# Gate and up chunks of the feed-forward in pairs, by seven block products in place of eight

## The reference

```python
def swiglu(h, w_gu, w_down):                 # h 256 x 1024, w_gu 1024 x 5632, w_down 2816 x 1024
    gate, up = jnp.split(h @ w_gu, 2, axis=-1)
    return (jax.nn.silu(gate) * up) @ w_down
x = x + 0.5 * swiglu(rmsnorm(x, ffn1_norm[i]), ffn1_w_gu[i], ffn1_w_down[i])
```

## Time and profile before

| | us |
|---|---|
| median of 3 runs | 2894.26 (2892.33 to 2895.02) |
| span of the profiled execution | 2891.6 |
| PE busy | 2851.9 |
| DVE busy | 1795.2 |
| ACT busy | 1578.0 |
| GpSimd busy | 452.6 |

### The profile page before, as it was taken

The page is one execution under the profiler, slowest core; times in us unless marked ns, Lnnn a source line. Parts: engine busy times, 40 slices in busy tenths (PEclk is TensorE's granted clock), DMA queues, the critical chain, the costliest instruction groups (busy, mean ns, idle before and its releaser), DMA issues.

```text
span 2891.6 us, 35970 instructions
## 1 busy us (share of the span) xinstructions
PE 2851.9 (99%) x14255; PEld 2419.0 (84%) x14255; DVE 1795.2 (62%) x2190; ACT 1578.0 (55%) x1982; POOL 452.6 (16%) x700
## 2 busy tenths in 40 slices
PE   9999999999999999999999999999999999999998
PEld 7888888888988888878888898888888888888887
DVE  5558666565666556466556487566675665775664
ACT  5448854544554454565444388643566463566462
POOL 1203512021002112041202107121000020000020
PEclk9999999999999999999999999999999999999999
DMA  8764267576548677537767653476645686645684
GB/s 277 234 191 129 88 218 239 195 247 214 173 155 245 214 227 238 181 117 225 227 207 241 200 159 117 133 247 212 200 147 174 214 278 220 194 146 176 217 278 158
DMA packets 397047, 574.90 MB, mean 199 GB/s; under 512 B 20016, under 2 KB 248624, under 8 KB 396880
## 3 DMA queue, kind: packets, MB, share of 16 engines
q1 hardware_dynamic: 372624, 508.62, 54.7%
q0 software_dynamic: 23680, 62.95, 7.0%
q10 hardware_dynamic: 576, 1.05, 0.1%
HBM read 540.03 MB, written 32.51 MB: 198 GB/s over the span
## 4 chain that ended last, share of the span: by engine, by line
PE 87%; DVE 6%; ACT 4%; issue 1%; DMA 1%; SPq 0%; POOL 0%; DVEq 0%; ACTq 0%
PE ps L430 26%; PE ps L432 26%; PE ps L431 26%; PE ps L616 2%; DVE lo L656 2%; DVE qkv L1609 2%; PE ps L503 1%; PE ps L505 1%; PE ps L504 1%; ACT goz L1400 1%; PE ps L587 1%; ACT hi L638 1%; PE ps L603 1%; ACT sl L1400 1%; ACT qkv L1400 0%
## 5 line engine op out<-in xcount | busy, mean ns | idle before, releaser
L656 DVE TENSOR_TENSOR lo<-raw,hi 128x2048 fp32r<-128x2048 f32 (+3 forms) x473 | 1052.6, 2238 | 451.0 <-ACT hi L638 451.0
L638 ACT ACTIVATE hi<-raw 128x2048 fp32r<-128x2048 f32 (+2 forms) x487 | 907.4, 1871 | 766.6 <-DMA raw<-in_ffn_w_gu 283.7
L430 PE MATMUL ps<-hi,xh 128*128 128x512 f32 (+1 forms) x2208 | 865.8, 392 | 3.3 <-DVE xl L812 2.4
L432 PE MATMUL ps<-hi,xl 128*128 128x512 f32 (+1 forms) x2208 | 858.4, 389 | 0.0
L431 PE MATMUL ps<-lo,xh 128*128 128x512 f32 (+1 forms) x2208 | 857.8, 388 | 0.0
L430 PEld LDWEIGHTS ps<-hi,xh 128*128 128x128 f32 x2208 | 415.0, 188 | 88.2 <-DVE lo L656 4.1
L432 PEld LDWEIGHTS ps<-hi,xl 128*128 128x128 f32 x2208 | 414.7, 188 | 85.8
L431 PEld LDWEIGHTS ps<-lo,xh 128*128 128x128 f32 x2208 | 415.1, 188 | 84.0 <-issue 1.0
L430 PE MATMUL ps<-hi,hhh 128*128 128x512 f32 x704 | 274.6, 390 | 0.0
L432 PE MATMUL ps<-hi,hhl 128*128 128x512 f32 x704 | 274.0, 389 | 0.0
L431 PE MATMUL ps<-lo,hhh 128*128 128x512 f32 x704 | 273.9, 389 | 0.0
(11 more groups left out here) (440 smaller groups left out, 3403.3 us busy)
## 6 DMA issues: line engine op xcount, KB each, us to landing
raw<-in_ffn_w_gu SPq DMA_DIRECT2D x348, 512.0 KB, 4.8
raw<-in_ffn_w_down SPq DMA_DIRECT2D x80, 1024.0 KB, 5.0
raw<-in_w_ff SPq DMA_DIRECT2D x64, 1024.0 KB, 5.4
raw<-in_w_in SPq DMA_DIRECT2D x60, 1024.0 KB, 5.1
raw<-in_gdn_w_in SPq DMA_DIRECT2D x32, 1024.0 KB, 5.5
turned<-hhf POOLq DMA_DIRECT2D x88, 256.0 KB, 4.5
hhr<-turned POOLq DMA_DIRECT2D x352, 64.0 KB, 4.0
raw<-in_sb_w_in SPq DMA_DIRECT2D x12, 1024.0 KB, 5.1
```

The lines of the kernel that those rows point to most:

```text
L430: e.matmul(o, a1, r1, start=kk == 0, stop=False)
L432: i = e.matmul(o, a2, r1, start=False, stop=kk == kts - 1)
L638: k.e.activation(k.m.hi[q % RING][:, 0:n], k.m.raw[q % RING][:, 0:n], ACT.Copy).then_inc(*k.up("act_piece_hi", ("hi", q)))
L656: k.e.tensor_tensor(m.lo[i][:, 0:n], m.raw[i][:, 0:n], m.hi[i][:, 0:n].bitcast(F32), ALU.subtract).then_inc(*k.up("dve_piece_lo", ("split" ...
```

## The change

Chunks n and n + 1 form a **pair**: (4, 5) in the first feed-forward stage, (2, 3) and (6, 7) in each of the other seven. For a pair, the input X (256 x 1024) is seen as 2 x 2 blocks and the weights W (1024 x 1024) as 2 x 2 blocks of 512 x 512 (in the code blocks `11` and `21` are the upper and lower input rows of chunk n + 1, `12` and `22` those of chunk n). The four blocks of the result come from seven block products and not from eight. Each product is 12 matmuls, and its weights count as one piece. In full:

- The four weight blocks are loaded into buffers of their own (`quad`, three in the stage's scratch and one over `lrow`), by `sync_quad`.
- GpSimd adds four sums of them, T1 = 11 + 12, T2 = T1 + 22, T4 = T2 + 21, T3 = 12 + 22 (`pool_sums`, 128 x 2048 each). T2 lies in the ring slot's `raw`, the others in place in `quad`.
- ACT and DVE split seven pieces for a pair (`scalar_high`, `vector_low`), where four were split for the same two chunks.
- Once per stage DVE and ACT make four sums of blocks of X and their high and low parts (`first`).
- ACT copies four PSUM results to SBUF (`keep`), DVE combines them with the later products (`whole`), and the gate of a pair then reads SBUF.
- The round trip of the hidden rows takes two chunks at once: `Flips(..., 1, 2)`; one buffer for turned rows in place of three; six sends and 24 fetches for a stage in place of 11 and 44. Sending and fetching are steps of their own on GpSimd, between the sums (`FFN_MID_POOL` and others).
- All word lists of the feed-forward are new. There are now four kinds of stage: first, next (`ffn1`, three stages), mid (`ffn2`, three stages) and last.

```diff
+        for cs in ffn_parts(g):
+            if len(cs) == 1:
+                self.rows(("gu", g, cs[0]), wgu, 0, 512, 8, chunk(cs[0]))
+            else:
+                self.quad(g, cs[0], {b: chunk(cs[2 - int(b[1])])(4 * int(b[0]) - 4, 4) for b in QUAD})
...
+QUAD = ("11", "12", "21", "22")
+SEVEN = ("11", "21", "T1", "T2", "T4", "22", "T3")
+SUMS = {"T1": ("11", "12"), "T2": ("T1", "22"), "T4": ("T2", "21"), "T3": ("12", "22")}
+IN_PLACE = {"11": "11", "T1": "11", "T3": "12", "22": "22", "21": "21", "T4": "21"}
+SUM_AFTER = {"T1": ("split", "11"), "T3": ("sum", "T2"), "T4": ("split", "21")}
+READERS = {"11": (("sum", "T2"), ("split", "T1")), "12": (("split", "T3"),), "22": (("sum", "T2"), ("sum", "T3"), ("split", "22")),
+           "21": (("split", "T4"),)}
+FFN_PAIRS_FIRST, FFN_PAIRS = (4,), (2, 6)
...
+def tensor_seven(k, plan, g, n, q):
+
+    m, e, seven, dims, S = k.m, k.e, plan.seven[g, n], (4, 2, 256), q["S"]
+    xs = lambda half, t: tuple((lambda kk, x=x: x[:, 4 * half + kk, t * P:(t + 1) * P]) for x in (m.xh, m.xl))
+    ss = lambda j: tuple((lambda kk, x=x: x[:, j, kk, :]) for x in S)
+    a, c, d, b = (("seven", g, n, j) for j in range(4))
+    for o, bank, left, first, last, after in (
+            ("11", a, xs(0, 0), True, False, ()), ("21", b, xs(1, 0), True, True, ()), ("T1", c, ss(0), True, False, (("S", g),)),
+            ("T2", a, ss(1), False, False, (("kept", g, n, "11"),)), ("T4", d, xs(1, 1), True, True, ()),
+            ("22", c, ss(3), False, True, (("kept", g, n, "T1"),)), ("T3", a, ss(2), False, True, (("kept", g, n, "T2"),))):
+        p = seven[o]
+        to = k.take(*bank) if first else k.bank(*bank)
+        if first:
+            k.wait_ge(*to.before)
+        for event in after:
+            k.wait_ge(*event)
+        k.wait_ge("split", p)
+        wh, wl = m.ring(m.hi, p, dims), m.ring(m.lo, p, dims)
+        out = to.ps[:, :].rearrange("p (a b) -> p a b", a=2)
+        for kk in range(4):
+            a1, a2 = left[0](kk), left[1](kk)
+            e.matmul(out, a1, wh[:, kk], start=first and kk == 0, stop=False, skip_group_check=True)
+            e.matmul(out, a1, wl[:, kk], start=False, stop=False, skip_group_check=True)
+            i = e.matmul(out, a2, wh[:, kk], start=False, stop=kk == 3, skip_group_check=True)
+        i.then_inc(*k.up("pe_proj", ("prod", g, n, o), ("used", p)))
+        if last:
+            k.close(to)
+        yield
...
+def scalar_high(k, plan, q):
+    g, n, o = plan.kind[q]
+    m, i = k.m, q % RING
+    src = ffn_room(m)["quad"][IN_PLACE[o]] if o in IN_PLACE else m.raw[i]
+    k.wait_ge("used", q - RING)
+    k.wait_ge(*(("sum", q) if o in SUMS else ("quad", g, n, o)))
+    k.e.activation(m.hi[i][:, :], src[:, :], ACT.Copy).then_inc(*k.up("act_piece_hi", ("hi", q)))
...
+def vector_low(k, plan, q):
+    g, n, o = plan.kind[q]
+    m, i = k.m, q % RING
+    src = ffn_room(m)["quad"][IN_PLACE[o]] if o in IN_PLACE else m.raw[i]
+    k.wait_ge(*(("sum", q) if o in SUMS else ("quad", g, n, o)))
+    k.wait_ge("hi", q)
+    if o == "T2":
+        k.wait_ge("sum", plan.seven[g, n]["T4"])
+    k.e.tensor_tensor(m.lo[i][:, :], src[:, :], m.hi[i][:, :].bitcast(F32), ALU.subtract).then_inc(*k.up("dve_piece_lo", ("split", q)))
...
+def pool_sums(k, plan, g):
+
+    m = k.m
+    for n in ffn_pairs(g):
+        seven = plan.seven[g, n]
+        for o in ("T1", "T2", "T4", "T3"):
+            p, quad = seven[o], ffn_room(m)["quad"]
+            raw = lambda o: quad[IN_PLACE[o]] if o in IN_PLACE else m.raw[seven[o] % RING]
+            k.wait_ge(*((SUM_AFTER[o][0], seven[SUM_AFTER[o][1]]) if o in SUM_AFTER else ("used", p - RING)))
+            for b in SUMS[o]:
+                k.wait_ge(*(("sum", seven[b]) if b in SUMS else ("quad", g, n, b)))
+            one, two = (raw(b) if b in SUMS else quad[b] for b in SUMS[o])
+            k.e.tensor_tensor(raw(o)[:, :], one[:, :], two[:, :], ALU.add).then_inc(*k.up("pool_sum", ("sum", p)))
+            yield
...
 def ffn_room(m):
     r = Room(m)
-    return dict(f=Flips(m, r, "hh", 11, 2, 2, 3), sg=[r(f"sg{i}", [P, 256]) for i in range(4)])
+    f = Flips(m, r, "hh", 11, 2, 2, 1, 2)
+    low = at + 11 * 2048
+    sg = [r(f"sg{i}", [P, 256]) for i in range(4)]
+    kept = {"T2": m.tensor("kU", [P, 512], F32, at + 6 * 2048), "T1": m.tensor("kc", [P, 512], F32, low + 8 * 2048),
+            "11": m.tensor("kA", [P, 512], F32, r.top - 4096), "T4": m.tensor("kd", [P, 512], F32, r.top - 2048)}
+    quad = {b: r(f"quad{b}", [P, PIECE]) for b in ("11", "12", "22")}
+    quad["21"] = m.tensor("quad21", [P, PIECE], F32, m.at_lrow)
+    return dict(f=f, sg=sg, kept=kept, quad=quad, gx=m.tensor("gx", [P, 8, S], F32, at + 2 * 2048),
+                S=(m.tensor("Sh", [P, 4, 4, P], F32R, at + 7 * 2048), m.tensor("Sl", [P, 4, 4, P], F32R, low + 9 * 2048)),
+                raw=m.tensor("Sr", [P, 4, 4, P], F32, low + 9 * 2048))
...
+FFN_MID_DVE = """
+W x1 S W S gate W flip S W gate flip W W W W whole W whole W whole whole W gate W gate W flip flip turn gate W W
+flip gate flip W W W W whole W whole turn W whole whole W W gate W gate flip flip turn W gate W flip gate flip W
+turn W gate flip W turn W W turn W W W out W W W W W W next out out
+"""
...
+FFN_MID_POOL = """
+sum sum sum sum send fetch sum send sum sum sum send fetch fetch send fetch send fetch send fetch
 """
...
+    def keep():
+        for n in ffn_pairs(g):
+            for o, bank in (("11", 0), ("T1", 1), ("T2", 0), ("T4", 2)):
+                b = k.bank("seven", g, n, bank)
+                k.wait_ge("prod", g, n, o)
+                if o in ("11", "T4"):
+                    for c, t in ffn_half_users(g, n, 0 if o == "11" else 1):
+                        k.wait_ge("hidden", g, c, t)
+                elif n != ffn_pairs(g)[0]:
+                    c = ffn_pairs(g)[ffn_pairs(g).index(n) - 1]
+                    k.wait_ge("hidden", g, c, 0 if o == "T2" else 1)
+                k.e.activation(r["kept"][o][:, :], b.ps[:, :], ACT.Copy).then_inc(
+                    *k.up("act_kept", ("kept", g, n, o), *([b.read] if o == "T4" else [])))
+                yield
...
+    def whole():
+        for n in ffn_pairs(g):
+            c0, c1 = n, n + 1
+            for o, done, bank, c, t in (("11", "21", 3, c1, 0), ("T2", "22", 1, c0, 0), ("T1", "T3", 0, c0, 1), ("T4", "T3", 0, c1, 1)):
+                b, s = k.bank("seven", g, n, bank), r["kept"][o][:, :]
+                k.wait_ge("prod", g, n, done)
+                k.wait_ge("kept", g, n, o)
+                if o == "T1":
+                    k.e.tensor_tensor(s, s, b.ps[:, :], ALU.subtract).then_inc(*k.up("dve_whole", ("whole", g, c, t)))
+                elif o == "T2":
+                    k.e.tensor_tensor(s, b.ps[:, :], s, ALU.subtract).then_inc(*k.up("dve_whole", ("whole", g, c, t), b.read))
+                else:
+                    k.e.tensor_tensor(s, s, b.ps[:, :], ALU.add).then_inc(*k.up("dve_whole", ("whole", g, c, t), b.read))
+                yield
...
+            k.e.tensor_tensor(gx[:, part, :], m.xh[:, part, :].bitcast(F32), m.xl[:, part, :].bitcast(F32), ALU.add).then_inc(*up(("gx", g, half)))
...
+        k.e.tensor_tensor(raw[:, 0], A(1, 0), A(1, 1), ALU.subtract).then_inc(*up(("S1", g)))
+        k.e.tensor_tensor(raw[:, 2], A(0, 0), A(1, 0), ALU.subtract).then_inc(*up())
...
+        k.e.tensor_tensor(raw[:, 1], raw[:, 0], A(0, 0), ALU.subtract).then_inc(*up(("S2", g)))
...
+        k.e.tensor_tensor(raw[:, 3], A(0, 1), raw[:, 1], ALU.add).then_inc(*up(("Sr", g)))
...
+        k.e.tensor_tensor(r["S"][1][:, :, :, :], raw[:, :, :, :], r["S"][0][:, :, :, :].bitcast(F32), ALU.subtract).then_inc(*up(("S", g)))
...
+def sync_quad(k, plan, g, n, b, mixer):
+
+    before = [x for x in plan.seven if x < (g, n)]
+    if before and ffn_pairs(g)[0] != n:
+        for what, o in READERS[b]:
+            k.wait_ge(what, plan.seven[before[-1]][o])
+    elif mixer:
+        for t in range(2):
+            for s in range(2):
+                k.wait_ge("res", g, t, s)
+    view = ffn_room(k.m)["quad"][b][:, :].rearrange("p (a u f) -> p a u f", a=4, u=2)
+    for j, (index, src) in enumerate(plan.quads[g, n][b]):
+        k.e.dma_start(view[index], src).then_inc(*k.up(f"dma_quad{b}", *([("quad", g, n, b)] if j else []), by=16))
```

303 lines of the change are left out of this document (215 added, 88 removed).

## The result

The changed kernel takes **3055.78 us** (median, 3051.64 to 3058.67) where the kernel before took 2893.3 beside it: ratio **1.0561, 95% interval 1.0548 to 1.0575**. The profiled execution has a span of 3054.7 us, 163.1 over the 2891.6 of before. The forecast was 2993, range 2915 to 3060.

The account below looks back on a forecast made before the run. PE was taken to bound the kernel. Pair costs of 90 us, saving included, plus 9 for the clock gave +99 on the 2891.6 us span, 2990.6, hence a median of 2993 us, range 2915 to 3060.

Parts of the forecast that it names:

- Removed: On PE, fifteen pairs save 180 matmuls of 0.227 us, 40.8 us, all on the path; the shared round trip brings nothing.
- Exclusion for a whole instruction: DVE work with two SBUF inputs and GpSimd's tensor work, 4.6 us a sum, shut each other out for whole instructions.
- The bounds, +8.8 and +21 a stage: From chunk 0 to chunk 8's first matmul, at least +8.8 us a stage (+61.6 for seven), at most +21 (+147).
- The first pair: First pair of a two-pair stage: splits come late as engines take turns, +8 us in mid, +6 in next.
- The second pair, +5: Second pair of a two-pair stage, without X work: T2's split comes 3 to 8 us late, +5 us.
- The first stage's pair, +5: The first stage's only pair was taken to cost the same as another stage's second pair, +5 us.
- Idle time: PE's idle time was to grow to about 170 us in the profile after.
- The clock, 9 us: After the 10 us gap at T1, slower matmuls cost about 1.3 us beyond DVE's lag, in seven stages: 9 us.
- Sums on DVE: Eight sums on DVE would hold the ports 18.3 us, not 36.8, and the budget would close, 77.5 against 81.7.
- Signs: Profile after: PE busy falls some 40 us, its waits on line 748 are 100 or more, new splits average about 3.
- the first (sums slip into gaps): Sums and splits alternate without harm in DVE's idle time, leaving only the saving: 2853 us; chance 0.10.
- The fourth, 3077: Slower than the upper bound: nothing hides and every pair pays the clock, +183 us, 3077; chance 0.06.

Follow-up runs that it names:

- run 6: The kernel before with only the two-chunk round trip of inner rows, no pairs of chunks: 2892.39 us, ratio 0.9998.
- run 1: The changed kernel with each GpSimd sum replaced by two fills of the same destination, which read no SBUF: 2895.02 us, ratio 1.0005.
- run 5: The changed kernel with each GpSimd sum replaced by three fills, together about as long as a sum (4.6 us): 2922.14 us, ratio 1.0103.
- run 11: The changed kernel without the sums of X and their split; products with T1, T2, T3 and 22 read blocks of X: 3001.33 us, ratio 1.0376.
- run 4: The changed kernel with the four sums of a pair on DVE and none on GpSimd: 2995.16 us, ratio 1.035.
- run 7: The changed kernel with only sums T4 (as 21 + 22) and T3 of each pair, 30 sums instead of 60: 2926.18 us, ratio 1.0114.
- run 9: The changed kernel with the four sums of a pair made by accumulating transfers instead of GpSimd's adder: 3193.13 us, ratio 1.1035.
- run 10: As run 9, with the products of T4 and T2 changing places: 3159.01 us, ratio 1.0924.

## Why the prediction was right in kind and short in size

The direction, the place and the mechanism hold; the time was 63 us short, 4 us inside the end of the range. Some 24 of them are idle time of PE, and some 40 its busy time. Step by step:

- **Removed.** 180 matmuls were put at 40.8 us. Without sums PE is busy 36.8 less, and the kernel gains 26: the rest of the additions costs some 10. The round trip is worth nothing (run 6). Right.
- **Exclusion for a whole instruction.** Right: every duration in the second stage's pair is work plus the rest of the other engine's instruction, and fills, which read nothing, disturb no split (runs 1 and 5). It can be worse than I read: the split of 11.49 us waited for two whole sums. The rule of the Trainium skill, "SBUF — State Buffer", "Who interferes with whom", holds here: with sums the split of T2 takes 5.08 us in the mean, with fills at most 2.30.
- **The bounds, +8.8 and +21 a stage**, clock apart: counted from the end of one down projection to the first matmul of the next, against before, the first stage loses 10.8 us, the stages next 17.3 to 19.2, mid and last 22.8 to 24.7. The last pass the upper bound by less than a stage's clock, 38.7 / 8 = 4.8. For the seven stages with two pairs the bounds held; my +11 and +13 within them were low, by the clock more than by the waits, as follows. The first stage, with one pair, had no bounds, and got twice its +5.
- **The first pair.** T1's split ended 17.1 us into the pair (423.37 less 406.25, where PE starts it), I had 15.8, and the gap of 10 us at T1 is there: 10.41. In the stages next, where the list puts the X work ahead, T1 is in time and the gap is at T2, as forecast. By PE's waits alone, less the 2.7 us saved, these pairs cost +6.4 to +6.5 (next) for my +6, and +8.7 to +10.6 (mid, last) for my +8. What I missed in the latter is block 21, which I had in time: PE waits 1.0 to 1.2 us for its split, since DVE's sums of X (5.11 and 5.09 us for 0.69 each) wait out T1's and T2's; and up to 1.7 us at the next ordinary piece. With the clock such first pairs run 33.4 to 35.9 us (mid, last) and 30.2 to 31.6 (next), where 21.8 was the length before.
- **The second pair, +5.** Right, clock apart: waits of 7.6 to 8.8 us, less 2.7, are +4.9 to +6.1. With the clock these pairs run 29.2 to 32.0 us. T2 is 6.0 to 7.6 us late, in my range of 3 to 8, and runs 5 and 11 show by what: its split waits for T4's sum, and then loses the turn to T3's.
- **The first stage's pair, +5.** This is one step that failed. By its waits (1.76 and 11.17 us, less 2.7) it costs +10, and it runs 33.9 us: T1's split stands through two sums there, and PE waits for it. I had taken it to be like a second pair, without a schedule of its own.
- **Idle time.** The terms imply 41 + 90 = 131 us more idle PE; it is 155. Short by 24: some 6 in the first pairs of the stages mid and last, 5 in the first stage, 4 in the other pairs. Most of the rest is the other additions, which I put at nothing: without any sum PE idles 48.7 us, 9 more than before.
- **The clock, 9 us.** The step that failed most: PE's busy time is 49 above the term removed, 38.7 of it in slow products. The size for one gap was about right, the count was not. I charged one gap a stage, that at T1, with 1.3 us after DVE's lag. There are five such gaps; their products are 1.4 to 2.3 us slow, and DVE's lag hides part of that, as I had it. At the gap shown T1's slow product is over at 427.84; without the loss it would be at 426.23, and T2's split ends at 427.14, so some 0.6 of 1.6 us is left; in the five it is 0.6 to 1.5. But there are 18 slow products, not 7: the other 13 stand at T2 (ten) and at block 21 (three), where the next split ends before even a fast product would, and the whole 1.4 to 2.3 us show. My own figure of 2.4 us for twelve matmuls, times 15 pairs, would have given 36.
- **Sums on DVE.** The budget "would close at 77.5 against 81.7" was wrong. It leaves out DVE's other work: with the 12.2 us that my upper bound names it is 89.7, which does not close. Even that is only 8 us a stage, and run 4 lost 128 us to the run without sums; the rest is DVE's own idle time in front of splits (66.2 us for ACT's high parts) and slower matmuls (33 us in the block products). The advice of the Trainium skill, "GPSIMD Engine Reference", "Engine selection", is borne out by 61 us, but even so the kernel is 3.5% slower than before.
- **Signs.** PE's busy time was to fall by some 40 us, and rose by 8.3: the same miss as the clock's. PE's waits on line 748 were to be 100 us or more: 143.4. Mean of the new splits about 3: 3.27, (267.0 + 76.3) / 105; single ones of 5 to 7, and one of 11.49. Idle about 170: 194.5. Waits on copies, loads and sends, to which I gave nothing: none among PE's longest; a load stands behind part of the 6.7 us ahead of ordinary pieces.

The rivals: the first (sums slip into gaps) needed excluded work under 76 us; two sums a pair, with 77, already cost 59 us, and so did not come true even there. The fourth, 3077, which I gave 0.06, was nearer than the forecast: it charged the clock 2.4 us for each of 15 pairs, 36 in all, where 38.7 came in the products and 49 in busy time; its waits were 33 us too many, 147 where 155 - 41 = 114 came. So it came near in part because two of its errors, 33 too many and 13 too few, cancel.

What stays open: the clock's term is read off the slow products, and no run has the gaps without it; why fills make PE wait ahead of ordinary pieces; and whether T4 made without T2, at the price of one more addition a pair, gives back the 45 us of the chain. That was not tried with GpSimd's sums. The bound by the run without sums is 2867: with sums that cost nothing the change would win 26 us of 2893.

## What to carry to other kernels

An engine that is 16% busy is not a free engine. Before work is moved to it, find in the trace whether its operations and those of the engine that feeds the critical one shut each other out, and count both as one engine over the stretch between two fixed points. Then count the chain: an operation that writes over its source waits for every other reader of it, here two sums and the split that they feed became three sums and the split. And a stall on PE costs more than its length: here 155 us more of idle time came with 38.7 us in slower block products, of which DVE's lag hid little.

## What I had not expected of the hardware

- GpSimd's fill of 128 x 2048 takes 1.81 us beside splits of 2.29 us; both are undisturbed. Only the sums, with two operands in SBUF, take turns with DVE.
- When both engines have such work waiting, each mostly waits out one instruction of the other: in run 11 T2's split took 6.1 to 6.5 us in the 15 pairs (some 4.2 waiting and 2.3 work), in run 7 GpSimd's sums 6.3 in the mean (1.7 waiting and 4.6 work), and shortening the one's instruction moves the waiting to the other. It isn't a strict alternation: in the changed kernel one split of DVE, which started first by the trace, waited for two sums in a row, 11.49 us.
- An accumulating transfer of 128 x 2048 floats within SBUF took 12.2 us to land in run 9 and 9.8 in run 10 (medians, beside the loads), where each 512 KB half of a block's load takes 8.7.
